# Triangular inverse in 32-column diagonal blocks, its last level as one block, and the triangular product in two parts

## The chip, the cores and the metric

The kernel runs on one core of a Trainium2 chip. The metric is the device time of one launch in microseconds, from the first to the last instruction of the program on that core. Five engines work side by side: TensorE (PE) multiplies matrices and writes to PSUM banks, VectorE (DVE), ScalarE (ACT) and GpSimd (POOL) copy and combine, SyncE (SP) issues the transfers. Each engine takes its instructions in their order and waits on semaphores.

## The reference, cut to what matters

Two layers of a hybrid decoder are run for a prompt of 256 tokens and for 8 samples of 4 tokens: a gated mixing layer with a dense SwiGLU, then an RWKV-7 layer with a top-2-of-8 expert SwiGLU. The change is in the RWKV-7 recurrence, 16 heads of width 64:

```python
def step(s, inp):
    r_t, w_t, k_t, v_t, kk_t, a_t = inp
    s_kk = jnp.einsum("bhij,bhj->bhi", s, kk_t)
    s = (s * w_t[:, :, None, :]
         - s_kk[..., None] * (kk_t * a_t)[:, :, None, :]
         + v_t[..., None] * k_t[:, :, None, :])
    y = jnp.einsum("bhij,bhj->bhi", s, r_t)
    return s, y
```

The kernel doesn't step token by token. It cuts the 256 tokens into four chunks of 64. Within a chunk, the dependence of a token on the tokens before it is a strictly triangular 64x64 matrix per head, and the sequence of steps becomes a product with the inverse of (identity minus that matrix).

## The kernel before, in words

All of the work of this stage stands on one list, `steps`, which every engine's program walks in the same order, each taking its own part of a step. Chunks 0 and 1 lie together as half `i=0`: chunk 0 on partitions 0 to 63 and chunk 1 on partitions 64 to 127; chunks 2 and 3 are half `i=1`. All matrices are 4-byte floats. Each product of the program appears in the trace as two MATMUL records, each with its own weight load.

- `score`: PE makes the products of keys and queries (L1640), DVE masks them into `MS` (L1154). `MS[:, BL]` is the triangular matrix.
- `xt0`: DVE writes the first diagonals into `XT`, the transposed inverse, which starts as the identity (L1162, two instructions of 128 partitions by 512).
- `x0`: PE transposes `XT` into `X` (L1651), ACT copies it out (L801).
- Levels m = 1 to 5 (blocks of 2, 4, 8, 16 and 32) double the size of the diagonal blocks that are inverted: `t1` multiplies the triangular matrix by X (L1663), ACT copies the result to `T1` (L808), `xl` multiplies by X and its transpose (L1678), and DVE writes what belongs to the level over X and XT under a mask (L1170, COPY_PREDICATED). The heads go in two groups of 8, `f` = 0 and 1, so that the engines overlap. Every product is 64x64 by 64x64, in pairs: one for partitions 0 to 63, one for 64 to 127.
- For each chunk c = 0 to 3: `w1` (L1692, L1700), then `u`, which multiplies the inverse by W1 (L1724), then `s` and `y` (L1742, L1751 to L1757). `u` alternates the 64x64 product of its own chunk with a 64x64 product on the other 64 partitions (L1711, L1716), which is needed anyway.

Between two steps of this chain stands one step of the `fill` list: scores of the second half, the same computation for the 32 sample tokens (names that begin with `q_`, some of them 32x32 products: L1779, L1786, L1793), and state updates (`q_s0` L1807, `q_qs` L1816, `q_st` L1865 and L1874).

```python
for i in range(2):
    if i:
        then(("x0", 1))
    for m in range(1, 6):
        then(("t1", i, m))
        then(("xl", i, m))
for c in range(4):
    for kind in ("w1", "u", "s", "y"):
        then((kind, c))
```

The inner line of `u`, for the eight head pairs p of each parity `h2`:

```python
mm = t.matmul(banks[2 + h2][cs, 64 * p:64 * p + 64], XT[cs, i, 2 * p + h2, :], W1[cs, h2, p, :], ...)
...
other(p, 1 - e)
```

After this stage follow the group norm, the output projection (L1913), the routing, and the experts (L1981), which stream 277 MB of weights.

Of the kernel before, what the change touches and what calls it, by code (L numbers as in the profile page):

```python
# [24 lines left out]
I32 = mybir.dt.int32  # L25
# [29 lines left out]
def trunk_kernel(nc, a, out):  # L55

    with ExitStack() as ctx:
# [128 lines left out]
        lvl = view(CHN + 5376, 768, "p (l x t) -> p l x t", l=6, x=2)  # L186
# [6 lines left out]
        id64 = view(CHN + 7200, 64)  # L193
        mskS = view(CHN + 7424, 2 * SMP, "p (r t) -> p r t", parts=2 * SMP, r=2)
# [12 lines left out]
        SB = slice(SMP, 2 * SMP)  # L207
        wkvo = view(CHN + 1024, 512, "p (c j) -> p c j", c=DC)
# [197 lines left out]
        def x_count(i, m, f, x):  # L406

            return 18 * i + 4 * (m - 1) + (2 * f + x if m < 5 else f) + 1
# [41 lines left out]
        def _(sp):  # L450
# [24 lines left out]
            for st in steps:  # L475
                if st == ("xl", 1, 5):
                    sp.wait_ge(S["t1_ready"], 20)
                    stream(len(pieces) - 5, len(pieces) - 4)
# [48 lines left out]
        def _(pool):  # L527
# [60 lines left out]
            step(g.tensor_tensor(lvl, lvlW[:, :, :, 0:64], lvlW[:, :, :, 64:128], ALU.add))  # L588
            step(g.tensor_tensor(id64, ident[:, 0:64], ident[:, 64:128], ALU.add))

# [13 lines left out]
            g.tensor_copy(XT, bc(id64, 1, [P, 2 * H, 64]).rearrange("p (i h) t -> p i h t", i=2)).then_inc(S["masks"], 1)  # L604
            pool.wait_ge(S["masks"], 2)
            g.tensor_copy(XTq[SB], bc(id64[SB, SMP:2 * SMP], 1, [SMP, H, SMP])).then_inc(S["masks"], 1)
# [74 lines left out]
        def _(act):  # L681
# [113 lines left out]
            for st in steps:  # L795
                k = st[0]
                if k == "x0":
                    i = st[1]
                    for f in range(2):
                        act.wait_ge(S["xt_tr"], 2 * i + f + 1)  # L800
                        s_.activation(X[:, 8 * f:8 * f + 8, :], banks[1 + 3 * f][:, :].rearrange("p (h t) -> p h t", h=8),  # L801
                                      ACT.Copy).then_inc(S["x0_ready"], 1)
                elif k == "t1":
                    _, i, m = st
                    n = 5 * i + m - 1
                    for f in range(2):
                        act.wait_ge(S["t1_ready"], 2 * n + f + 1)
                        s_.activation(T1[:, f], banks[3 * f][:, :].rearrange("p (h t) -> p h t", h=8), ACT.Copy) \  # L808
                            .then_inc(S["t1_done"], 1)
# [136 lines left out]
        def _(dve):  # L946
# [200 lines left out]
            for st in steps:  # L1147
# [9 lines left out]
                elif k == "xt0":  # L1157
# [3 lines left out]
                    for f in range(2):  # L1161
                        v.copy_predicated(XT[:, i, 8 * f:8 * f + 8, :], bc(lvl[:, 0, 1, :], 1, [P, 8, 64]).bitcast(I32),  # L1162
                                          MS[:, BL, i, 8 * f:8 * f + 8, :]).then_inc(S["xt0_ready"], 1)
                elif k == "xl":
                    _, i, m = st
                    for f in range(2):
                        for x in range(0 if m < 5 else 1, 2):
                            dve.wait_ge(S["x_ready"], x_count(i, m, f, x))
                            dst = XT[:, i, 8 * f:8 * f + 8, :] if x else X[:, 8 * f:8 * f + 8, :]
                            v.copy_predicated(dst, bc(lvl[:, m, x, :], 1, [P, 8, 64]).bitcast(I32),  # L1170
                                              banks[1 + 3 * f + x][:, :].rearrange("p (h t) -> p h t", h=8)) \
# [30 lines left out]
                elif k == "q_xt0":  # L1202
                    q_wait(dve, "q_ms", 1)
                    v.copy_predicated(XTq[SB], bc(lvl[SB, 0, 1, SB], 1, [SMP, H, SMP]).bitcast(I32), MSq[SB, :, 0, :]) \
                        .then_inc(S["q_dve"], 1)
                elif k == "q_x2":
                    g_ = st[1]
                    q_wait(dve, "q_x2", g_)
                    v.copy_predicated(XTq[SB, 8 * g_:8 * g_ + 8, :], bc(lvl[SB, 1, 1, SB], 1, [SMP, 8, SMP]).bitcast(I32),
# [185 lines left out]
        def _(pe):  # L1395
# [229 lines left out]
            for st in steps:  # L1625
# [19 lines left out]
                elif k == "x0":  # L1645
                    i = st[1]
                    for f in range(2):
                        pe.wait_ge(S["xt0_ready"], 2 * i + f + 1)
                        for j in range(8):
                            for ch in BOTH:  # L1650
# [417 lines left out]
```

## Time and profile before

| | |
|---|---|
| time, median of 3 runs | 1684.76 us (1683.76 to 1685.39) |
| the profiled execution | 1685.16 us, span 1683.3 us |
| PE busy | 1588.4 us (94%) |
| DVE, ACT, POOL busy | 61%, 46%, 5% |
| scores to `x0` of the first half | 614.4 to 621.3 us |
| inverse, both halves | 621.3 to 697.2 us |
| the four chunks' products | 697.2 to about 756 us |
| experts | from 884 us |

A matmul's end is modelled in the trace and its records overlap, so rates of PE are read from the starts of consecutive rows, not from their durations. PEclk is the granted TensorE clock as a share of 2.4 GHz: 1.00 is 2.4 GHz, 0.50 is 1.2 GHz.

### The profile page before, as it was taken

Reading aid. Unit: us, or ns where it says so; the run is one execution under the profiler, and the core shown is the slowest. Engines: PE = TensorE matmul, PEld = TensorE weight load, DVE = VectorE, ACT = ScalarE, POOL = GpSimd, SP = SyncE. Lnnn points to the kernel's source line nnn. Section 1 sums busy time; section 2 is a strip of 40 time slices with the busy share of each in tenths; the row PEclk is TensorE's granted clock in tenths of the full one; section 3 lists DMA queues with packets and bytes.
Section 4 is the critical chain, followed back from the end, with each engine's and each line's share of the span. In section 5 each row is a group of like instructions: output and inputs, shape, how many; then the busy total and the mean of one; then the engine's idle time right before and its main releaser. Section 6 shows DMA issues by size and latency. Waiting matters only on the chain.

```text
span 1683.3 us, 25991 instructions
## 1 busy us (share of the span) xinstructions
PE 1588.4 (94%) x11388; PEld 1258.0 (75%) x11388; DVE 1030.5 (61%) x981; ACT 780.3 (46%) x724; POOL 88.4 (5%) x140
## 2 busy tenths in 40 slices
PE   6999989999989999998869999999999999999991
PEld 5777769999957779995656777777777777777771
DVE  2243134544363645314357888888888888888883
ACT  1120034443331422222026777777777777777771
POOL 2300000000000001232000000000000000000001
PEclk9999999999989999986879999999999999999996
DMA  8443345545333220113039999999999999999963
GB/s 252 130 126 100 107 151 161 164 144 145 104 101 126 75 52 4 32 37 98 25 122 382 404 384 380 367 382 352 379 376 373 376 372 377 365 382 356 379 253 96
DMA packets 238282, 378.28 MB, mean 225 GB/s; under 512 B 27385, under 2 KB 141289, under 8 KB 226610
## 3 DMA queue, kind: packets, MB, share of 16 engines
q1 hardware_dynamic: 232370, 367.19, 62.5%
q0 software_dynamic: 2000, 6.04, 1.2%
q10 hardware_dynamic: 3792, 3.30, 0.6%
q8 instruction: 92, 1.51, 0.4%
q14 instruction: 28, 0.23, 0.0%
HBM read 368.34 MB, written 8.17 MB: 224 GB/s over the span
## 4 chain that ended last, share of the span: by engine, by line
PE 91%; DVE 5%; DMA 2%; issue 1%; ACT 1%; POOL 0%; ACTq 0%; POOLq 0%; DVEq 0%; SPq 0%
PE bank L1981 44%; PE bank L1486 13%; PE bank L1433 8%; PE bank L1532 6%; PE bank L1479 4%; PE bank L1913 2%; PE bank L1678 2%; PE bank L1991 1%; PE bank L1663 1%; PE bank L1470 1%; PE bank L1874 1%; DVE arena L336 1%; PE bank L1865 1%; PE bank L1922 0%; PE bank L1555 0%
## 5 line engine op out<-in xcount | busy, mean ns | idle before, releaser
L1285 DVE TENSOR_TENSOR wL<-ering,wH 128x2048 fp32r<-128x2048 f32 x264 | 604.4, 2290 | 100.1 <-ACT wH L882 95.0
L882 ACT ACTIVATE wH<-ering 128x2048 fp32r<-128x2048 f32 x264 | 506.0, 1917 | 154.9 <-PE bank L1981 154.8
L1981 PE MATMUL bank<-wH,xgH 128*96 128x512 f32 (+1 forms) x768 | 291.0, 379 | 1.2 <-DVE xgL L1292 1.2
L1981 PE MATMUL bank<-wH,xgL 128*96 128x512 f32 (+1 forms) x768 | 288.2, 375 | 0.0
L1981 PE MATMUL bank<-wL,xgH 128*96 128x512 f32 (+1 forms) x768 | 287.8, 375 | 0.0
L1981 PEld LDWEIGHTS bank<-wH,xgH 128*96 128x96 f32 x768 | 126.1, 164 | 44.1 <-DVE xgL L1292 1.5
L1981 PEld LDWEIGHTS bank<-wH,xgL 128*96 128x96 f32 x768 | 124.5, 162 | 44.8
L1981 PEld LDWEIGHTS bank<-wL,xgH 128*96 128x96 f32 x768 | 124.7, 162 | 42.4
L1981 PE MATMUL bank<-wH,hH 128*96 128x512 f32 x352 | 139.3, 396 | 0.0
L1981 PE MATMUL bank<-wH,hL 128*96 128x512 f32 x352 | 138.4, 393 | 0.0
L1981 PE MATMUL bank<-wL,hH 128*96 128x512 f32 x352 | 137.8, 392 | 0.0
L1433 PE MATMUL bank<-arena 128*128 128x288 f32 x512 | 129.4, 414 | 1.2 <-DVE arena L974 1.2
L1028 DVE TENSOR_TENSOR fwL<-fring,fwH 128x2048 fp32r<-128x2048 f32 (+1 forms) x38 | 76.3, 2011 | 80.7 <-ACT fwH L725 80.7
L1433 PEld LDWEIGHTS bank<-arena 128*128 128x128 f32 x512 | 98.4, 194 | 28.5 <-DVE arena L974 1.4
L1532 PE MATMUL bank<-arena 128*128 128x288 f32 (+2 forms) x448 | 112.6, 414 | 1.5 <-DVE arena L1081 1.5
L725 ACT ACTIVATE fwH<-fring 128x2048 fp32r<-128x2048 f32 (+1 forms) x38 | 64.0, 1684 | 104.9 <-DMA fring<-f_w_gate 60.7
L1486 PE MATMUL bank<-fxH,fwH 128*128 128x288 f32 x352 | 105.0, 298 | 7.0 <-DVE fxL L1036 7.0
L1532 PEld LDWEIGHTS bank<-arena 128*128 128x128 f32 (+2 forms) x448 | 82.8, 186 | 30.5 <-issue 4.3
L1486 PE MATMUL bank<-fxH,fwL 128*128 128x288 f32 x352 | 104.5, 297 | 0.0
L1486 PE MATMUL bank<-fxL,fwH 128*128 128x288 f32 x352 | 104.1, 296 | 0.0
L1981 PEld LDWEIGHTS bank<-wH,hL 128*96 128x96 f32 x352 | 56.7, 161 | 24.7
L1981 PEld LDWEIGHTS bank<-wL,hH 128*96 128x96 f32 x352 | 56.9, 162 | 23.0
(342 smaller groups left out, 2018.1 us busy)
## 6 DMA issues: line engine op xcount, KB each, us to landing
ering<-m_w_gate SPq DMA_DIRECT2D x88, 1024.0 KB, 7.7
ering<-m_w_up SPq DMA_DIRECT2D x88, 1024.0 KB, 8.3
ering<-m_w_down SPq DMA_DIRECT2D x88, 1024.0 KB, 7.6
arena<-a_w_in SPq DMA_DIRECT2D x16, 1024.0 KB, 5.4
arena<-b_w_rkv SPq DMA_DIRECT2D x12, 1024.0 KB, 5.1
fring<-f_w_gate SPq DMA_DIRECT2D x11, 1024.0 KB, 5.2
fring<-f_w_up SPq DMA_DIRECT2D x11, 1024.0 KB, 5.3
fring<-f_w_down SPq DMA_DIRECT2D x16, 704.0 KB, 4.7
```

The costliest lines, as they stand in the source:

```text
L336: nc.vector.scalar_tensor_tensor(out=dst[:, c, :], in0=xT[:, c, :], scalar=vec[:, gain + c:gain + c + 1], in1=rinv[:, :], op0=ALU.mult, op ...
L725: nc.scalar.activation(fwH[:, n % FRING, 0:w], fring[:, (F_GU + n) % RING, 0:w], ACT.Copy) \
L882: s_.activation(wH[:, g % HRING, :], ering[:, g % MRING, :], ACT.Copy).then_inc(S["e_hi"], 1)
L1028: v.tensor_tensor(fwL[:, n % FRING, 0:w], fring[:, (F_GU + n) % RING, 0:w], fwH[:, n % FRING, 0:w].bitcast(F32), ALU.subtract).then_inc(S[ ...
L1285: v.tensor_tensor(wL[:, g % HRING, :], ering[:, g % MRING, :], wH[:, g % HRING, :].bitcast(F32), ALU.subtract).then_inc(S["e_lo"], 1)
L1433: mm = t.matmul(banks[g_ % 4][:, 0:T], w[:, k, P * j:P * j + P], hT[:, k, :], start=(k == 0), stop=(k == DC - 1))
L1479: mm = t.matmul(banks[c % 4][:, 0:T], w[:, k, :], vT[:, k, :], start=(k == 0), stop=(k == AC - 1))
L1486: mm = t.matmul(bank[:, 0:T], w2[l], x2[r][:, k, :], start=(start and m == 0), stop=(stop and m == 2))
L1532: mm = t.matmul(bank, w(k), x[:, k, :], start=(k == 0), stop=(k == ks - 1))
L1678: mm = t.matmul(banks[1 + 3 * f + x][ch, 64 * j:64 * j + 64], pair[x], pair[1 - x], start=(j == 0), stop=True, skip_group_check=True)
L1913: mm = t.matmul(banks[c % 4][:, 0:T], w[:, k, P * j:P * j + P], yT[:, k, :], start=(k == 0), stop=(k == DC - 1))
L1981: mm = t.matmul(dst, lhs[l], rhs[r], start=(start and m == 0), stop=(stop and m == 2), skip_group_check=True)
```

## The change

The inverse is kept as two 32x32 diagonal blocks per chunk and head. `XT`, `X` and `T1` are half as wide, and in levels 1 to 4 every 64x64 product becomes two 32x32 products, one for each block; with both chunks that is a round over the four quarters of 32 partitions. Level 5 computes the one off-diagonal block: `t1` is 32 products (32x32), `xl` writes that block and, through the identity, the lower diagonal block side by side into one bank, and DVE copies both in one instruction to the new `XR`. The product `u` is cut in two: rows 0 to 31 of the chunk take a 32x32 product with `XT`, rows 32 to 63 a product of 64 rows by 32 columns with `XR`. `xt0` becomes four instructions of 32 partitions by 512, and PE waits for all four before `x0`. Masks and the counts of the semaphores follow. The samples' steps use a 32-wide identity and are otherwise the same. `steps` is the same list.

```diff
-        XT = view(B[0], 2 * D, "p (i h t) -> p i h t", i=2, h=H)
-        X = view(B[0] + 2048, D, "p (h t) -> p h t", h=H)
-        T1 = view(B[0] + 3072, D, "p (f h t) -> p f h t", f=2, h=8)
+        XT = view(B[0], D, "p (i h t) -> p i h t", i=2, h=H)
+        XR = view(B[0] + 1024, D, "p (i h t) -> p i h t", i=2, h=H)
+        X = view(B[0] + 2048, 512, "p (h t) -> p h t", h=H)
+        T1 = view(B[0] + 2560, 512, "p (h t) -> p h t", h=H)
...
-                    for f in range(2):
-                        v.copy_predicated(XT[:, i, 8 * f:8 * f + 8, :], bc(lvl[:, 0, 1, :], 1, [P, 8, 64]).bitcast(I32),
-                                          MS[:, BL, i, 8 * f:8 * f + 8, :]).then_inc(S["xt0_ready"], 1)
+                    for k4, rows in enumerate(QUARTERS):
+                        o = 32 * (k4 % 2)
+                        v.copy_predicated(XT[rows, i], bc(lvl[rows, 0, 1, :], 1, [32, H, 32]).bitcast(I32),
+                                          MS[rows, BL, i, :, o:o + 32]).then_inc(S["xt0_ready"], 1)
...
+                    if m == 5:
+                        dve.wait_ge(S["x_ready"], x_count(i, 5, 0, 1))
+                        v.tensor_copy(XR[:, i], banks[2][:, :].rearrange("p (h t) -> p h t", h=H)).then_inc(S["x_done"], 1)
+                        continue
...
                         for j in range(8):
-                            for ch in BOTH:
-                                mm = t.matmul(banks[3 * f][ch, 64 * j:64 * j + 64], MS[ch, BL, i, 8 * f + j, :], X[ch, 8 * f + j, :],
-                                              start=(j == 0), stop=True, skip_group_check=True)
+                            for k4, rows in enumerate(QUARTERS):
+                                o = 32 * (k4 % 2)
+                                mm = t.matmul(banks[3 * f][rows, 32 * j:32 * j + 32], MS[rows, BL, i, 8 * f + j, o:o + 32],
+                                              X[rows, 8 * f + j, :], start=(j == 0), stop=True, skip_group_check=True)
...
-                                for ch in BOTH:
-                                    pair = (XT[ch, i, 8 * f + j, :], T1[ch, f, j, :])
-                                    mm = t.matmul(banks[1 + 3 * f + x][ch, 64 * j:64 * j + 64], pair[x], pair[1 - x],
+                                for rows in QUARTERS:
+                                    pair = (XT[rows, i, 8 * f + j, :], T1[rows, 8 * f + j, :])
+                                    mm = t.matmul(banks[1 + 3 * f + x][rows, 32 * j:32 * j + 32], pair[x], pair[1 - x],
                                                   start=(j == 0), stop=True, skip_group_check=True)
...
+                    for j in range(H):
+                        for lhs, to in ((T1, 0), (id32, 32)):
+                            for ch in (0, 64):
+                                rows = slice(ch + 32, ch + 64)
+                                mm = t.matmul(banks[2][ch + to:ch + to + 32, 32 * j:32 * j + 32],
+                                              lhs[rows, j, :] if to == 0 else lhs[rows], XT[rows, i, j, :],
+                                              start=(j == 0), stop=True, skip_group_check=True)
...
                         for p in range(DC):
-                            mm = t.matmul(banks[2 + h2][cs, 64 * p:64 * p + 64], XT[cs, i, 2 * p + h2, :], W1[cs, h2, p, :],
+                            lo, hi = slice(64 * e, 64 * e + 32), slice(64 * e + 32, 64 * e + 64)
+                            t.matmul(banks[2 + h2][lo, 64 * p:64 * p + 64], XT[lo, i, 2 * p + h2, :], W1[lo, h2, p, :],
+                                     start=(p == 0), stop=True, skip_group_check=True)
+                            mm = t.matmul(banks[2 + h2][hi, 64 * p:64 * p + 64], XR[cs, i, 2 * p + h2, :], W1[cs, h2, p, :],
                                           start=(p == 0), stop=True, skip_group_check=True)
                             if p == DC - 1:
                                 mm.then_inc(S["u_ready"], 1)
                             other(p, 1 - e)
```

**A level on PE.** What stands on PE for `t1` and `xl` of the third level of the first half, before (a row gives the bank written, the rows by columns of the output, and the count of equal products behind one another):

```order
L1663 MATMUL bank0<-arena 64x64 x16
L1663 MATMUL bank3<-arena 64x64 x16
L1678 MATMUL bank1<-arena 64x64 x16
L1678 MATMUL bank2<-arena 64x64 x16
L1678 MATMUL bank4<-arena 64x64 x16
L1678 MATMUL bank5<-arena 64x64 x16
```

and now, at the same place:

```order
L1679 MATMUL bank0<-arena 32x32 x32
L1679 MATMUL bank3<-arena 32x32 x32
L1694 MATMUL bank1<-arena 32x32 x32
L1694 MATMUL bank2<-arena 32x32 x32
L1694 MATMUL bank4<-arena 32x32 x32
L1694 MATMUL bank5<-arena 32x32 x32
```

A level of 96 products is one of 192 smaller ones, in the same order of banks.

**The product `u` on PE.** The start of `u` of chunk 0 and its end before; bank 2 and 3 take the product for even and odd heads, banks 4 and 5 the products on the other 64 partitions:

```order
L1840 MATMUL bank7<-arena 32x64 x8
L1724 MATMUL bank2<-arena 64x64
L1711 MATMUL bank4<-arena 64x64
L1724 MATMUL bank2<-arena 64x64
L1711 MATMUL bank4<-arena 64x64
...
L1724 MATMUL bank3<-arena 64x64
L1716 MATMUL bank5<-arena 64x64
L1711 MATMUL bank4<-arena 64x64 x8
```

and now:

```order
L1879 MATMUL bank7<-arena 32x64 x8
L1761 MATMUL bank2<-arena 32x64
L1763 MATMUL bank2<-arena 32x64
L1747 MATMUL bank4<-arena 64x64
L1761 MATMUL bank2<-arena 32x64
L1763 MATMUL bank2<-arena 32x64
L1747 MATMUL bank4<-arena 64x64
...
L1763 MATMUL bank3<-arena 32x64
L1752 MATMUL bank5<-arena 64x64
L1747 MATMUL bank4<-arena 64x64 x8
```

Each of the 16 rounds of a chunk has three products of three sizes (32x32, 64x32 and 64x64 of the array: L1761 has 32 rows of input, L1763 has 64) where it had two of one size.

**`xt0` on DVE.** The second half's `xt0` (L1162) between the masks of the last scores (L1154), the copies of level 3 (L1170) and the samples' first step (L1204), before:

```order
L1154 TENSOR_TENSOR arena<-bank6,arena 128x2x4x64
L1154 TENSOR_TENSOR arena<-bank7,arena 128x2x4x64
L1162 COPY_PREDICATED arena<-arena 128x512 x2
L1170 COPY_PREDICATED arena<-arena,bank1 128x512
L1170 COPY_PREDICATED arena<-arena,bank2 128x512
L1170 COPY_PREDICATED arena<-arena,bank4 128x512
L1170 COPY_PREDICATED arena<-arena,bank5 128x512
L1204 COPY_PREDICATED arena<-arena 32x512
```

and now (L1164, L1173, L1185 and L1219 are the same steps):

```order
L1164 TENSOR_TENSOR arena<-bank6,arena 128x2x4x64
L1164 TENSOR_TENSOR arena<-bank7,arena 128x2x4x64
L1173 COPY_PREDICATED arena<-arena 32x512 x4
L1185 COPY_PREDICATED arena<-arena,bank1 128x256
L1185 COPY_PREDICATED arena<-arena,bank2 128x256
L1185 COPY_PREDICATED arena<-arena,bank4 128x256
L1185 COPY_PREDICATED arena<-arena,bank5 128x256
L1219 COPY_PREDICATED arena<-arena 32x512
```

Two instructions have become four of the same length along the free axis; the copies of a level read and write half as much.

## Rows read from the trace of the kernel before

**Rows 1.** The page's chain of work that ended last, by engine and by line
```profile
PE 91%; DVE 5%; DMA 2%; issue 1%; ACT 1%; POOL 0%; ACTq 0%; POOLq 0%; DVEq 0%; SPq 0%
```

**Rows 2.** Busy time by stretch: A:B length, PE, PEld, DVE, ACT, POOL, then PEclk, DMA, GB/s
```profile
650.30:697.00 46.70, 46.70 (x1553) 46.15 (x1552) 17.59 (x25) 12.63 (x23) 4.17 (x4) 1.00 0.05 15
697.00:734.30 37.30, 37.30 (x1030) 34.52 (x1024) 7.91 (x13) 10.69 (x18) 15.14 (x8) 1.00 0.16 36
...
737.80:741.10 3.30, 3.30 (x72) 3.30 (x70) 0.69 (x1) 0.65 (x2) 1.04 (x1) 0.50 0.02 5
741.30:748.00 6.70, 6.70 (x197) 6.58 (x193) 2.08 (x3) 0.98 (x2) 2.09 (x2) 1.00 0.01 2
748.10:761.60 13.50, 12.82 (x129) 9.98 (x129) 0.29 (x1) 2.37 (x4) 0.53 (x1) 0.50 0.54 175
```

**Rows 3.** Groups of instructions by line, 620 to 702 us: count, busy us, mean ns
```profile
L1678 PE MATMUL bank<-arena 64*64 64x64 f32 x1152 | 35.5, 218 | 0.0
...
L1663 PE MATMUL bank<-arena 64*64 64x64 f32 x640 | 20.8, 219 | 0.2
...
L1651 PE MATMUL bank<-arena 64*64 64x64 f32 x128 | 5.4, 256 | 2.6 <-DVE arena L1162 2.6
```

**Rows 4.** Timeline of PE, 661 to 678 us: start us, length us, what, weights' rows*columns
```profile
669.70 0.69 PE L1779 MATMUL bank<-arena 32*32 32x32 f32 x16
670.31 2.08 PE L1663 MATMUL bank<-arena 64*64 64x64 f32 x64
672.23 1.10 PE L1807 MATMUL bank<-arena 64*64 64x64 f32 x32
673.16 3.90 PE L1678 MATMUL bank<-arena 64*64 64x64 f32 x128
676.99 0.69 PE L1786 MATMUL bank<-arena 32*32 32x32 f32 x16
```

**Rows 5.** Timeline of PE around `u` of chunk 0
```profile
702.20 0.27 PE L1724 MATMUL bank<-arena 64*64 64x64 f32 x1
702.20 0.27 PE L1711 MATMUL bank<-arena 64*64 64x64 f32 x1
...
704.05 0.22 PE L1724 MATMUL bank<-arena 64*64 64x64 f32 x1
704.06 0.22 PE L1716 MATMUL bank<-arena 64*64 64x64 f32 x1
```

**Rows 6.** Timeline of PE, 785 to 800 us, where sizes alternate
```profile
790.13 1.17 PE L1901 MATMUL bank<-arena 128*128 128x288 f32 x2
791.23 1.32 PE L1902 MATMUL bank<-arena 32*128 32x288 f32 x2
792.48 1.33 PE L1897 MATMUL bank<-arena,halves 128*128 128x288 f32 x2
793.60 1.17 PE L1901 MATMUL bank<-arena 128*128 128x288 f32 x2
```

**Rows 7.** Timeline of PE, 811.3 to 816.2 us, where the clock is 0.50
```profile
810.75 5.88 PE L1913 MATMUL bank<-arena 128*128 128x288 f32 x12 [4.31 <-issue]
```

**Rows 8.** Timeline of PE, 613 to 625 us
```profile
614.37 3.72 PE L1640 MATMUL bank<-arena 64*64 64x128 f32 x128 [0.64 <-DVE arena L1146]
618.02 0.65 PE L1767 MATMUL bank<-arena 64*32 64x64 f32 x32
621.27 3.34 PE L1651 MATMUL bank<-arena 64*64 64x64 f32 x64 [2.60 <-DVE arena L1162]
```

**Rows 9.** Timeline of DVE, 620 to 653 us
```profile
620.49 1.34 DVE L1162 COPY_PREDICATED arena<-arena 128x512 f32<-128x512 int32 x2
...
641.75 3.60 DVE L1162 COPY_PREDICATED arena<-arena 128x512 f32<-128x512 int32 x2
645.25 2.55 DVE L1170 COPY_PREDICATED arena<-arena,bank 128x512 f32<-128x512 int32 x4
```

**Rows 10.** Timeline of POOL, 640 to 651 us
```profile
640.51 8.53 POOL L611 TENSOR_TENSOR arena<-arena 32x1024 f32<-32x1024 f32 x4 [24.06 <-PE bank L1640]
```

More of the change, by code:

```diff
@@ L193, in trunk_kernel @@
         id64 = view(CHN + 7200, 64)
+        id32 = view(CHN + 7264, 32)
         mskS = view(CHN + 7424, 2 * SMP, "p (r t) -> p r t", parts=2 * SMP, r=2)
@@ L207, in trunk_kernel @@
         SB = slice(SMP, 2 * SMP)
+        QUARTERS = [slice(32 * k, 32 * k + 32) for k in range(4)]
         wkvo = view(CHN + 1024, 512, "p (c j) -> p c j", c=DC)
@@ L406, in x_count, with t_count @@
         def x_count(i, m, f, x):
-            return 18 * i + 4 * (m - 1) + (2 * f + x if m < 5 else f) + 1
+            return 17 * i + (4 * (m - 1) + 2 * f + x + 1 if m < 5 else 17)
+        def t_count(i, m, f):
+            return 9 * i + (2 * (m - 1) + f + 1 if m < 5 else 9)
         def expert_load(sp, rd, g):
@@ L804, in _ @@
                     _, i, m = st
-                    n = 5 * i + m - 1
-                    for f in range(2):
-                        act.wait_ge(S["t1_ready"], 2 * n + f + 1)
-                        s_.activation(T1[:, f], banks[3 * f][:, :].rearrange("p (h t) -> p h t", h=8), ACT.Copy) \
-                            .then_inc(S["t1_done"], 1)
+                    for f in range(2 if m < 5 else 1):
+                        hs_ = slice(8 * f, 8 * f + 8) if m < 5 else slice(0, H)
+                        act.wait_ge(S["t1_ready"], t_count(i, m, f))
+                        s_.activation(T1[:, hs_, :], banks[3 * f][:, 0:256 if m < 5 else 512].rearrange("p (h t) -> p h t", t=32),
+                                      ACT.Copy).then_inc(S["t1_done"], 1)
                 elif k == "w1":
@@ L1646, in _ @@
                     i = st[1]
+                    pe.wait_ge(S["xt0_ready"], 4 * i + 4)
                     for f in range(2):
-                        pe.wait_ge(S["xt0_ready"], 2 * i + f + 1)
                         for j in range(8):
-                            for ch in BOTH:
-                                mm = t.matmul(banks[1 + 3 * f][ch, 64 * j:64 * j + 64], XT[ch, i, 8 * f + j, :], id64[ch],
+                            for rows in QUARTERS:
+                                mm = t.matmul(banks[1 + 3 * f][rows, 32 * j:32 * j + 32], XT[rows, i, 8 * f + j, :], id32[rows],
                                               start=(j == 0), stop=True, skip_group_check=True)
                         mm.then_inc(S["xt_tr"], 1)
-                elif k == "t1":
+                elif k == "t1" and st[2] < 5:
                     _, i, m = st
@@ L1685, in _ @@
                     if c == 0:
-                        pe.wait_ge(S["x_done"], 36)
+                        pe.wait_ge(S["x_done"], 34)
                         mm = w1_value(0)
@@ L1778, in _ @@
                     for j in range(8):
-                        mm = t.matmul(banks[7][SB, 32 * j:32 * j + 32], XTq[SB, 8 * g_ + j, :], id64[SB, SB],
+                        mm = t.matmul(banks[7][SB, 32 * j:32 * j + 32], XTq[SB, 8 * g_ + j, :], id32[SB],
                                       start=(j == 0), stop=True, skip_group_check=True)
```

49 lines of the change are left out of this document (32 added, 17 removed).

## The prediction, made before the run

> **What bounds the kernel now.** I read the chain that ended last first: it is PE for 91% of the span [rows 1], so what the change adds to PE or takes from it counts, unless PE waits there. Then the stretches of this stage: from 650.3 to 697 us PE is busy for all 46.70 of 46.70 us, and so it is from 697 to 734 us, while DVE has 17.59 and ACT 12.63 us of work in the first of them [rows 2]. So ACT and DVE are covered there, and their smaller copies gain nothing by themselves. The experts behind this stage are on PE's chain too, so a shift here is a shift of the end. The sum is made against the profiled execution, 1685.16 us, 0.4 us above the median of the runs.
>
> **Levels: PE's products.** Before, L1678, L1663 and L1651 have 1152 + 640 + 128 = 1920 records [rows 3]. Their rate is read from starts: L1807 begins at 672.23 and L1678 at 673.16, 0.93 us for 32 records [rows 4], which is 29 ns a record or 58 ns for a pair (one record on each half of the array's rows). 960 pairs at 58.3 ns are 56 us. The change has 3712 records: `x0` 256, `t1` and `xl` of levels 1 to 4 1024 + 2048, level 5 128 + 256. How fast four 32x32 products on four quarters go isn't in the trace, since all its 32x32 products use one quarter. Those take 0.61 us for 16 records from 669.70 to 670.31, a change of size among it; the row's own length less one record's 0.19 leaves 0.50 us for 15 intervals, 32 ns or so [rows 4]. If four quarters run beside one another as two halves do, a round of four records takes that 32 ns. 3584 records in rounds of four are 896, the 128 of the last `t1` are 64 pairs: 960 x 32 ns = 31 us. The gain is 25 us. The other bound is an issue limit. The fastest records of the trace are L1767's, four tiles at a time: 32 in 0.65 less 0.22 us, 14 ns each, but for 32 records only; over 128 records L1640 needs 618.02 - 614.37 = 3.65 us, 28.5 ns each [rows 8]. At 28.5 ns the 3712 records take 106 us, a loss of 50. I take the gain of 25 us, since L1767 shows that products in different tiles do run together, and keep the loss for the range.
>
> **Changes of tile size.** The chip charges for them. L1678 at 673.16 has 128 records, 3.73 us at 58.3 ns a pair, and the next row starts 3.83 us later, 0.10 more. L1779's 16 records take 0.61 where 16 x 32 ns are 0.51. L1663's 64 records take 1.92 where 32 pairs are 1.87 [rows 4]. From 64x64 to 32x32 and back is 0.26 us, 0.13 a change. It holds for single products: L1901, L1902 and L1897 alternate 128-row and 32-row weights, two records each, and a round from 790.13 to 793.60 takes 3.47 us [rows 6]; six records at L1913's 0.49 us (5.88 us for 12 [rows 7]) are 2.94 at most, so two changes cost 0.53, 0.27 each, at half the clock, as 0.13 is at the full one. The Trainium skill, TensorEngine Tiling (Array Packing), "Key Properties", says the same against this change: "Changing tiling mode (not just tile) drains the TensorE". By the page, as by the rows, `u` pays at each product; it gives no price, the rows do.
>
> Around the levels few changes are new: the fill steps of 64x64 now break runs of 32x32, while the samples' 32x32 steps no longer break runs of 64x64. Along PE's order the count goes from 157 to 358, 192 of the 201 new ones in `u`, 9 elsewhere: 1 us.
>
> **The product `u`, where I expect the loss.** Before, L1724 alternates with L1711 or L1716 on the other half of the rows, from 702.20 to 704.11 us for 16 rounds [rows 5]: 0.117 us a round, 4 records, 64 rounds in all. Now a round has 32x32, 64x32 and 64x64 behind one another: six records of 64 columns, none beside another, 6 x 58 = 0.35 us, and three changes of 0.13, together 0.74 us. At the full clock that is 0.62 x 64 = 40 us more. ACT's and DVE's copies behind `u` were hidden by PE work and stay so; nothing else gets shorter.
>
> It won't stay at the full clock, I think. In this same stage the clock is 0.50 from 737.8 to 741.1 us and again from 748.1 to 761.6 [rows 2], after PE had been issuing without a gap, but products of 8 columns or one tile at a time. `u` now uses between a sixteenth and a quarter of the array, with drains. At half the clock a round is 6 x 0.107 + 3 x (0.13 to 0.27), some 1.2 us. With seven rounds of a chunk's 16 at the full clock and nine at half, a chunk's `u` takes 5.2 + 10.8 = 16 us, 14 more than now, 56 us for four. The rest of the stage is about 46 us of PE work, 11 of it at half the clock already; if the clock comes back half-way through what lies between two `u`, it adds some 18 us. Together 75 us, between 40 (clock kept) and about 110 (clock low throughout: 64 x 1.1 + 35).
>
> **`xt0`.** DVE's two L1162 take 1.34 us at 620.49, and PE starts x0 at 621.27 with the first of them done [rows 9, 8]. Four of the same length on 32 partitions each take 0.61 us from start to start (1.34 less one's 0.73), and PE waits for the last: 3 x 0.61 = 1.8 us. In the second half the two took 3.60 us [rows 9], beside POOL's four L611 (8.53 us for four, 2.1 each [rows 10]); each of DVE's, which read SBUF twice, ended only behind one of POOL's. Four would end behind four: 2 x 2.1 = 4.3 us more, and the copies of level 3 (L1185) queue behind them, with PE's next `t1` behind those. PE has run ahead by then, so it waits for all of it. With PE's longer pauses I add 2 us of half clock: 8 us. This is 0 at least (if POOL and DVE don't meet) and 12 at most.
>
> **Sum.** -25 + 1 + 75 + 8 = +59 us: 1685.2 + 59 = 1744, say 1745 us.
>
> **The rivals.**
> - The clock holds: PE still issues without a pause in `u`, and from 650 to 734 us, where half the array or less was in use, it was 1.00 [rows 2]. Then -25 + 1 + 40 + 6 = +22: 1707 us. Against it stand the two stretches at 0.50.
> - An issue limit: the levels run at the 28.5 ns of L1640's 128 records, 75 us more than in the forecast: 1820 us. L1640's records have 128 columns, so their rate can come from their length, and that speaks against it. The Trainium skill, TensorEngine Tiling, "Instruction Overhead", has a rule for such a limit: some 60 cycles for each matmul, so that a tiling factor isn't to be taken from a dimension that is small already. This trace has records at 14 ns in four tiles, below those 25 ns, but not for long.
> - Faster: changes of size inside `u` cost nothing, because what drains is one tile's queue and not the array. Then `u` costs two further serial products a round, 0.117 x 64 = 7.5 us, and the sum is -25 + 1 + 6 + 7.5 = -10.5: 1674 us. It decides the sign when a change costs under about 0.05 us; rows 4 and 6 have 0.13 and more.
>
> **How the numbers follow.** Forecast 0.50 (its own range 1720 to 1775), clock holds 0.12, issue limit 0.24, faster 0.10, and 0.04 for mixtures near no change. 0.2% of the time (3.4 us) is about what a measurement tells from nothing. Faster 0.10, same 0.03, slower 0.87. From 1700 to 1830 us the range takes in the second case and most of the third; out are the faster one and the third's upper end.
>
> **What the profile after would show.** Right: in `u`, the 32-row, 64x32 and 64x64 records start some 60 and 150 ns apart in turn, each chunk's `u` is 12 to 18 us long, and PEclk falls to 0.50 in or behind it; in the levels, four records start within 32 ns and `t1` of a level takes about 1 us; DVE's second `xt0` spans about 8 us. Wrong: a `u` of 2 to 3 us, or a level's `t1` of 3.6 us, or PEclk 0.50 in the levels, which would make their gain nothing and the time up to 30 us longer than forecast.

## The result, and the profile after

The changed kernel takes 1805.9 us (median of 4 runs, 1804.0 to 1806.7) against 1684.3 us (1681.4 to 1685.4): 1.072 times as long, 95% interval 1.0705 to 1.0742. The forecast of slower was right; 1745 us was not: the loss is 121.6 us where 61 were forecast. The measured time lies within the range of 1700 to 1830 us.

The page's chain [rows 1] and its clock row:

```profile
PE 90%; DVE 5%; issue 3%; DMA 2%; ACT 0%; POOL 0%; ACTq 0%; POOLq 0%; DVEq 0%; SPq 0%
...
PEclk9999999999899965566668899999999999999996
```

PE bounds as before. New is that "issue", time in which PE waited for nothing that the profile shows, went from 1% to 3% of the span, and that the clock row reads 5 to 8 for nine slices (of 45 us each) in a row.

Line numbers move: `score` L1640 is now L1655, `x0` L1666, `t1` L1679 (level 5 L1702), `xl` L1694 (L1713), `u` L1761 (32x32) and L1763 (64x32), key and value L1747 and L1752, L1880 is L1919, `xt0` L1173.

Busy time by stretch (columns as in [rows 2]), first of the kernel before, x0 to the first `u` and from there to L1880, then the same two of the kernel after:

```profile
621.30:702.20 80.90, 79.41 (x2537) 77.68 (x2537) 39.52 (x55) 19.77 (x35) 12.46 (x8) 0.98 0.08 21
702.20:772.50 70.30, 67.80 (x1513) 59.47 (x1513) 10.16 (x16) 15.24 (x26) 26.87 (x16) 0.83 0.27 74
```
```profile
626.60:755.30 128.70, 91.59 (x4325) 84.28 (x4326) 32.14 (x54) 14.33 (x33) 12.76 (x8) 0.58 0.05 12
755.30:894.00 138.70, 136.03 (x1645) 101.97 (x1643) 10.24 (x17) 15.25 (x26) 26.89 (x16) 0.63 0.14 37
```

The first scores and x0, PE's timeline [rows 8]:

```profile
617.46 3.72 PE L1655 MATMUL bank<-arena 64*64 64x128 f32 x128 [0.64 <-DVE arena L1156]
...
626.61 1.79 PE L1666 MATMUL bank<-arena 32*32 32x32 f32 x128 [4.84 <-DVE arena L1173]
```

So the 121.6 us by which the two profiled spans differ (1683.3 and 1804.9) fall apart into:

| stretch | before | after | difference | forecast |
|---|---|---|---|---|
| up to the first score | 614.4 | 617.5 | +3.1 | 0 |
| first score to x0 | 6.9 | 9.2 | +2.3 | +1.8 |
| x0 to the first `u` | 80.9 | 128.7 | +47.8 | -25 + 1 + 6 = -18 |
| first `u` to L1880 / L1919 | 70.3 | 138.7 | +68.4 | +75 |
| from there to the end | 910.8 | 910.9 | +0.1 | 0 |

`u` costs about what was forecast. The levels were to gain and lost. The groups by line show how (they answer to [rows 3]), and so do the waits of PE from 610 to 755 us (us in total, times, longest):

```profile
L1694 PE MATMUL bank<-arena 32*32 32x32 f32 x2048 | 31.0, 226 | 25.1 <-issue 25.0
L1679 PE MATMUL bank<-arena 32*32 32x32 f32 x1024 | 16.8, 231 | 8.7 <-issue 8.7
```
```profile
PE bank L1694 <- issue: 25.0, 16, 2.8
PE bank L1679 <- issue: 8.7, 7, 1.8
PE bank L1666 <- DVE arena L1173: 4.8, 1, 4.8
```

In [rows 3] the levels' lines had 0.0 and 0.2 us of idle time. Now PE stands idle for 128.70 - 91.59 = 37.1 us of the stretch, 33.7 of it in 23 pauses in the levels for which no semaphore is to blame. PE's timeline in the levels:

```profile
656.64 1.93 PE L1679 MATMUL bank<-arena 32*32 32x32 f32 x128 [1.01 <-issue]
660.51 1.92 PE L1694 MATMUL bank<-arena 32*32 32x32 f32 x127 [1.93 <-issue]
663.94 2.05 PE L1694 MATMUL bank<-arena 32*32 32x32 f32 x128 [1.51 <-issue]
667.77 0.26 PE L1694 MATMUL bank<-arena 32*32 32x32 f32 x1 [1.78 <-issue]
667.78 1.93 PE L1679 MATMUL bank<-arena 32*32 32x32 f32 x127
671.51 0.25 PE L1679 MATMUL bank<-arena 32*32 32x32 f32 x1 [1.81 <-issue]
```

PE runs 128 records in 1.93 less one record's 0.25 us, 13 ns a record, stops for 1 to 2 us, and runs the next 128: one burst each 3.7 us ((671.51 - 656.64) / 4), whichever line they belong to. That is 29 ns a record on average. The transfers of the same kernel from 650 to 700 us (queue: packets, MB, share of 16 engines):

```profile
q8 instruction: 14, 0.23, 1.9%
```

These are 14 packets of 0.23 MB / 14 = 16 KB in 50 us, one each 3.6 us. A record and its weight load are two instructions; 128 such pairs are 256 instructions, and 16 KB are 64 bytes for each. That q8 carries PE's program shows in its packets over the whole run, first of the kernel before, then of the changed one:

```profile
q8 instruction: 92, 1.51, 0.4%
...
q8 instruction: 107, 1.75, 0.4%
```

Fifteen more packets are 3840 instructions, and PE has 1920 more records and 1920 more weight loads (13308 against 11388). So PE's program comes to it in portions while it runs, and in the levels PE uses up a portion in half the time in which the next one comes. At 29 ns the 4325 records of the stretch take 125 of its 128.7 us. In the kernel before the 2537 records of the stretch would take 74 us at this rate, less than its 80.9, and it has no such pause. The Trainium skill, Runtime: NRT & Kernel Launch, "Instruction fetch mechanics", describes the portions, "16 KiB blocks (256 instructions)", and says that fetching hides because instructions are issued more slowly than they arrive. The trace agrees with the first (16 KB a packet), and not with the second (33.7 us of pauses).

`u` at the full clock and at half, chunk 0:

```profile
756.77 0.29 PE L1761 MATMUL bank<-arena 32*32 32x64 f32 x2
757.00 0.30 PE L1763 MATMUL bank<-arena 64*32 64x64 f32 x2
757.22 0.33 PE L1747 MATMUL bank<-arena 64*64 64x64 f32 x2
757.48 0.29 PE L1761 MATMUL bank<-arena 32*32 32x64 f32 x2
...
763.73 0.41 PE L1761 MATMUL bank<-arena 32*32 32x64 f32 x2
764.07 0.42 PE L1763 MATMUL bank<-arena 64*32 64x64 f32 x2
764.42 0.47 PE L1752 MATMUL bank<-arena 64*64 64x64 f32 x2
764.82 0.41 PE L1761 MATMUL bank<-arena 32*32 32x64 f32 x2
```

A round takes 0.71 us at the clock of 1.00, then 1.09 us at 0.50; forecast were 0.74 and 1.2. Six records of 58 ns leave 0.36 us for three changes of size, 0.12 each; six of 107 ns leave 0.45, 0.15 each.

### The profile page after: what moved, and what is told of

Read it like the earlier page. It is cut to its first block, busy times and chain, and to the rows that moved or that the text cites. A ratio compares the mean times of both kernels' runs of the same rounds, so it can differ in the third digit from the quotient of the medians.

```text
span 1804.9 us, 29832 instructions
## 1 busy us (share of the span) xinstructions
PE 1669.0 (92%) x13308; PEld 1307.3 (72%) x13308; DVE 1025.5 (57%) x983; ACT 774.8 (43%) x722; POOL 87.5 (5%) x143
## 3 DMA queue, kind: packets, MB, share of 16 engines
q1 hardware_dynamic: 232370, 367.19, 58.3%
## 4 chain that ended last, share of the span: by engine, by line
PE 90%; DVE 5%; issue 3%; DMA 2%; ACT 0%; POOL 0%; ACTq 0%; POOLq 0%; DVEq 0%; SPq 0%
PE bank L2020 41%; PE bank L1501 12%; PE bank L1448 7%; PE bank L1547 5%; PE bank L1494 4%; PE bank L1952 2%; PE bank L1694 2%; PE bank L1763 1%; PE bank L2030 1%; PE bank L1761 1%; PE bank L1679 1%; PE bank L1747 1%; PE bank L1485 1%; PE bank L1752 1%; PE bank L1913 1%
## 5 line engine op out<-in xcount | busy, mean ns | idle before, releaser
L2020 PE MATMUL bank<-wL,hH 128*96 128x512 f32 x352 | 137.8, 392 | 0.0
```

What stands on the lines that cost most here:

```text
L2020: mm = t.matmul(dst, lhs[l], rhs[r], start=(start and m == 0), stop=(stop and m == 2), skip_group_check=True)
```

## The experiments

Two theories for the levels. **A**, supply: PE's instructions arrive 16 KB at a time (a portion), each 3.7 us or so, 29 ns for a record with its weight load. **B**, the products' own time, which is what they take with all their instructions there: PEclk is 0.58 in this stretch, and that, with the copies between levels, makes them long. The kernel before ran 1683.8 to 1685.2 us (medians) beside the experiments; ratios are against it.

**1. The levels alone (u_one).**

```diff
-    t.matmul(banks[2 + h2][lo, 64 * p:64 * p + 64], XT[lo, i, 2 * p + h2, :], W1[lo, h2, p, :], ...)
-    mm = t.matmul(banks[2 + h2][hi, 64 * p:64 * p + 64], XR[cs, i, 2 * p + h2, :], W1[cs, h2, p, :], ...)
+    mm = t.matmul(banks[2 + h2][cs, 64 * p:64 * p + 64], U1[cs, i, 2 * p + h2, :], W1[cs, h2, p, :], ...)
```

> The changed kernel with `u` as one 64x64 product a head again; its weights are then a 64-wide view of the memory that holds the diagonal and the upper blocks, so the values are not the inverse's. Levels, copies and all else stay. This gives the price of the split `u` by subtraction. By the forecast's term for `u` (+75 us, 56 inside the four `u` and 18 between them) the time falls to about 1731 us. In the trace of the changed kernel the stretch from the first `u` to L1919 is 138.7 us long against 70.3 before, so if all of that is the split, the time is 1737.5 us. If the low clock at the end of the levels, and not `u`, is what makes this stretch long, it stays above 1770 us.

1733.2 us, ratio 1.0284 (1.0265 to 1.0303). Its stretches, x0 to `u` and behind:

```profile
623.50:750.30 126.80, 90.31 (x4328) 83.09 (x4328) 32.25 (x54) 14.30 (x33) 12.75 (x8) 0.60 0.05 13
750.30:820.80 70.50, 67.75 (x1512) 59.54 (x1512) 10.16 (x16) 15.24 (x26) 26.87 (x16) 0.82 0.28 73
```

From `u` on it is the kernel before again (70.5 us, clock 0.82), so the low clock of the levels carries nothing over. The levels, `xt0` included, cost 48 us.

**2. `u` alone (u_split).**

```diff
-    mm = t.matmul(banks[2 + h2][cs, 64 * p:64 * p + 64], XT[cs, i, 2 * p + h2, :], W1[cs, h2, p, :], ...)
+    t.matmul(banks[2 + h2][lo, 64 * p:64 * p + 64], XT[lo, i, 2 * p + h2, 0:32], W1[lo, h2, p, :], ...)
+    mm = t.matmul(banks[2 + h2][hi, 64 * p:64 * p + 64], XT[cs, i, 2 * p + h2, 32:64], W1[cs, h2, p, :], ...)
```

> The kernel before with only `u` split, into a 32x32 product on the first 32 rows and a 64x32 product on all 64, both read from the 64-wide XT; the result is the reference's. If the split alone makes the loss behind the levels, the time is 1684 + 68 = 1752 us. The forecast's term says 1684 + 75 = 1759. If part of the loss in the changed kernel came from entering `u` at half the clock, it is less here, since before the clock is 1.00 up to `u`: the first `u` then loses about 6 us less, 1746 us.

1750.8 us, ratio 1.040 (1.0375 to 1.0425): the split alone costs 66 us. From its first `u` to L1883 it needs 138.2 us with the clock at 0.63, as the changed kernel does, though its levels ran at 0.98. So the clock at which `u` is entered changes nothing here either. The same products behind the first `u` don't take the same time in every kernel, though: in the profiled runs of the kernels with the split and alternating `u` this stretch is 134.4 to 142.8 us long (xt0_two and cols64), so a few us in the price of `u` are not explained. 48 + 66 = 114 of the 121.6 us; the rest was not separated (3.1 of them lie before the first score, and the two stretches of the profiled run of u_one and of this one are shorter by 1.9 and 0.5 us).

**3. Half the levels' records (two_quarters).**

```diff
-    for rows in QUARTERS:
+    for rows in QUARTERS[::2]:
```

> The changed kernel with x0 and levels 1 to 4 computed on the first and the third quarter of the rows alone: the other two quarters' products are left out, 3328 records become 1664. A round is then two records side by side where it was four, so its own time does not change. Theory A, supply of instructions: PE's instructions come 16 KB at a time, 20 packets and 0.33 MB in 74 us of the levels, and PE stops after each 128 records; then the levels need half the packets, 13 fewer of 3.7 us: 48 us less, 1758 us. Theory B, the clock of 0.50 and the copies that PE waits for between levels: rounds and waits stay, so the time stays within 5 us of 1806.

1772.3 us, ratio 1.0524 (1.0499 to 1.0548): 34 us less than the changed kernel. Its waits of PE, 615 to 720 us:

```profile
PE bank L1679 <- DVE arena L1185: 4.9, 1, 4.9
PE bank L1666 <- DVE arena L1173: 4.8, 1, 4.8
```

DVE's timeline before the first of these waits:

```profile
646.73 8.18 DVE L1173 COPY_PREDICATED arena<-arena 32x512 f32<-32x512 int32 x4
654.94 1.44 DVE L1185 COPY_PREDICATED arena<-arena,bank 128x256 f32<-128x256 int32 x4
```

The stretch x0 to `u`:

```profile
623.80:716.10 92.30, 87.33 (x2663) 83.33 (x2664) 31.97 (x54) 14.35 (x33) 12.75 (x8) 0.51 0.06 15
```

The pauses without a releaser are gone. Theory B's "unchanged" is refuted, theory A's 48 us are not reached: with the supply no longer in the way, PE is at the half clock nearly all through. It is busy for 87.33 us, more than the 77 us that 2663 records need at 29 ns, so the own time decides here. And it waits 4.9 us for L1185, the level's copies, which stand on DVE behind `xt0`'s 8.18 us. That is the wait which the forecast put into `xt0`'s term; in the changed kernel PE was held by its pauses and doesn't show it.

**4. Twice the columns (cols64).** `t1` and `xl` of levels 1 to 4 alike; shown is `xl`.

```diff
-    ... banks[1 + 3 * f + x][rows, 32 * j:32 * j + 32], pair[x], pair[1 - x], ...
+    ... banks[1 + 3 * f + x][rows, 64 * j:64 * j + 64], pair[x], wide[1 - x], ...
```

> The changed kernel with 64 columns instead of 32 in each product of levels 1 to 4: the moving operand also takes the neighbouring head, so the values are not the inverse's; as many instructions, twice the columns. Theory A, supply of instructions: 128 records of 64 columns in rounds of four take 32 x 58 ns = 1.9 us at the full clock and 3.4 us at half, less than the 3.7 us between packets, so the time stays within 5 us of 1806. Theory B, the products' own time at the half clock: 3072 records at 13.4 ns are 41 us and become 82, so the time is 1845 us.

1805.4 us, ratio 1.0712 (1.0694 to 1.0730): the same as the changed kernel, with twice the columns in 3072 records. Its stretch x0 to `u`, and two bursts:

```profile
623.80:752.20 128.40, 90.20 (x4325) 82.38 (x4325) 32.30 (x54) 14.30 (x33) 12.76 (x8) 0.89 0.05 12
```
```profile
694.50 1.98 PE L1697 MATMUL bank<-arena 32*32 32x64 f32 x127 [0.90 <-issue]
698.38 1.36 PE L1697 MATMUL bank<-arena 32*32 32x64 f32 x83 [1.90 <-issue]
```

It is 128.4 us against 128.7, at a mean clock of 0.89 against 0.58, and a burst begins 3.9 us after the last. Neither the columns nor the clock sets this stretch with all its records in place, and theory B's 1845 us are out. What is left is the number of records.

**5 and 6. Fewer columns in the kernel before, with the count kept and halved (b_cols32, b_one128).** `x0` and `t1` are changed in the same way as the `xl` shown.

```diff
-    mm = t.matmul(... 64 * j:64 * j + 64], pair[x], pair[1 - x], ...)
+    mm = t.matmul(... 64 * j:64 * j + 32], pair[x], pair[1 - x][:, 0:32], ...)   # b_cols32
```
```diff
-    for ch in BOTH:
-        pair = (XT[ch, i, 8 * f + j, :], T1[ch, f, j, :])
-        mm = t.matmul(banks[1 + 3 * f + x][ch, 64 * j:64 * j + 64], pair[x], pair[1 - x], ...)
+    pair = (XT[:, i, 8 * f + j, :], T1[:, f, j, :])
+    mm = t.matmul(banks[1 + 3 * f + x][0:64, 64 * j:64 * j + 32], pair[x], pair[1 - x][:, 0:32], ...)
```

> The kernel before with 32 columns instead of 64 in each product of x0 and of all levels: the right half of each 64x64 result is left out, the 1920 records stay. Theory A, supply of instructions: 16 KB, which is 128 records with their weight loads, reach PE each 3.7 us or so, 29 ns a record, and that is what the levels of the kernel before take already (58.3 ns a pair). So half the columns gain nothing: within 4 us of 1685. Theory B, the products' own time: a pair goes from 58.3 ns to the 32 ns of 32-column products, 960 pairs, 25 us less: 1660 us.

> As the kernel before, but in x0 and all levels one product of 128-row weights and 32 columns takes the place of the pair of 64-row products of 64 columns; the second chunk's results are left out. The 1920 records become 960. Theory A: the supply then allows 29 ns a record, 960 x 29 = 28 us, and their own time is 960 x 32 = 31 us, against 56 before: 25 us less, 1660 us, where the same halving of columns with the count kept gains nothing. Theory B (own time alone) says 1660 us here too; only the other kernel of this pair tells them apart. If 128-row weights of 32 columns cost more than 32 ns a record, less is gained.

Both expectations failed: 1705.8 us, ratio 1.0137 (1.0108 to 1.0165), and 1744.1 us, 1.0361 (1.0338 to 1.0384). Both are slower, clear of the noise, with less work. First rows of b_cols32, at the full clock and at half, then of b_one128 at half:

```profile
636.18 1.94 PE L1663 MATMUL bank<-arena 64*64 64x32 f32 x62
...
702.80 3.60 PE L1678 MATMUL bank<-arena 64*64 64x32 f32 x64
```
```profile
705.45 3.62 PE L1661 MATMUL bank<-arena 128*64 128x32 f32 x32
```

62 records in 1.94 less 0.22 us are 28 ns each, a pair 56 ns, as with 64 columns; at half the clock 64 records in 3.38 us are 53 ns, a pair 107. In b_one128 a record takes (3.62 - 0.25) / 31 = 109 ns, where 32 columns at half the clock were to take 64. Two records that follow each other in one tile are spaced by the 64 columns of their weights, not by the 32 that move. L1779, from which the forecast read its 32 ns, has weights of 32 columns. The Trainium skill, TensorE: Matmul & The Clock Gate, "LDWEIGHTS (loading the stationary operand)", says that a weight load takes its number of columns / 1.2 in ns; an estimate by it is 53 ns for 64 columns. The 56 ns at the full clock agree, the 107 at half are twice that. The loss goes with the clock: between x0 and `u` it is 0.74 in b_cols32 and 0.51 in b_one128, against 0.98. The pair says nothing on A, since a product's own time never fell.

**7 and 8. More instructions, no more work (b_waits, b_waits_long).**

```diff
+    for _ in range(9):                       # b_waits: ahead of each pair in the levels
+        pe.wait_ge(S["masks"], 2)
+    for _ in range(14):                      # b_waits_long: ahead of each product of L1433
+        pe.wait_ge(S["h_ready"], DC)
```

> The kernel before, with nine waits ahead of each pair of products in the levels, all on a semaphore that has long had its value: 1814 more instructions for PE there, and no other work. Theory A, supply of instructions (16 KB, 256 instructions, each 3.7 us): the levels stand at that limit already with 29 ns a record, so 1814 more are 7.1 portions more and the time grows by 26 us to 1710 us, with pauses of PE that show no releaser. Theory B: there is no such limit, the levels run at the products' own time, and a wait that is met is passed while products run: within 4 us of 1684.

> The control: the kernel before, with 1792 more met waits, this time seven for each product of L1433, whose 512 records of 288 columns take 411 ns each. Theory A: 128 records there take some 50 us, far longer than the 3.7 us a portion, so the extra seven portions are hidden: within 4 us of 1684. If a met wait costs PE's sequencer time that products don't hide, this kernel is slower as well, and the other one's loss says nothing on the supply.

1843.2 us, ratio 1.0943 (1.0923 to 1.0964), and 1753.0 us, 1.0408 (1.0388 to 1.0427). The control is slower too, so the pair says nothing for A. (Two waits share an instruction: fourteen are the seven that the expectation speaks of.) A met wait, one whose semaphore has its value already, costs PE 68 us / 1792 = 38 ns even ahead of products of 400 ns. Between the short ones the loss is 158 / 1814 = 87 ns for each, but that isn't the wait's price alone: the clock there is 0.53 from 650 to 700 us, against 1.00 in the kernel before. In b_waits, q8 brought fewer portions in 650 to 700 us than in the changed kernel, not more:

```profile
q8 instruction: 6, 0.10, 0.7%
```

**9. The products of `u` in another order (u_grouped).**

```diff
     for p in range(DC):
         t.matmul(banks[2 + h2][lo, ...], XT[lo, ...], W1[lo, h2, p, :], ...)
+    for p in range(DC):
         mm = t.matmul(banks[2 + h2][hi, ...], XR[cs, ...], W1[cs, h2, p, :], ...)
         ...
+    for p in range(DC):
         other(p, 1 - e)
```

> The changed kernel with the products of `u` in another order: for each half of the heads first the eight 32x32 ones, then the eight 64x32 ones, then the eight of key or value; the same products, some 24 changes of tile size where there were 192. In the trace of the changed kernel a round of `u` takes 0.705 us at the full clock, 0.36 of it in three changes, and 1.095 us at half, 0.45 of it in three changes: 0.12 and 0.15 us a change. If changes cost that, 168 fewer are 20 to 25 us: 1783 us. By the forecast's prices (0.13 to 0.27) it is 22 to 45 us less. If the drain belongs to the tile that changes and the loss is the serial products alone, the time stays at 1806 us.

1761.4 us, ratio 1.0469 (1.0444 to 1.0495): 44.5 us less than the changed kernel with the very same products. Its `u` and the stretch from the first `u` to the state transposes:

```profile
795.45 1.08 PE L1761 MATMUL bank<-arena 32*32 32x64 f32 x16
796.45 1.08 PE L1764 MATMUL bank<-arena 64*32 64x64 f32 x16
797.46 0.97 PE L1752 MATMUL bank<-arena 64*64 64x64 f32 x13
```
```profile
749.10:849.00 99.90, 96.86 (x1646) 85.97 (x1645) 10.16 (x16) 15.26 (x26) 26.89 (x16) 0.73 0.19 52
```

Sixteen records of a kind (eight products) take 1.00 us, 63 ns each, so a round is 0.38 us where it was 0.71. That is 21 us for 64 rounds at the full clock. The stretch is 38.8 us shorter; the rest of it goes along with the clock, 0.73 against 0.63, and was not measured apart. "The loss is the serial products alone" is refuted: most of it comes from alternating the sizes, by the changes themselves and by the lower clock together.

**10. The same order in the kernel before (b_u_grouped).** The diff is that of u_split, in the order of u_grouped.

> The kernel before with `u` split, its products grouped by tile size: eight 32x32, eight 64x32, eight of key or value, for each half of the heads. The result is the reference's. Split and alternating it was 1750.8 us. If grouping takes off what it took off in the changed kernel (44.5 us), the time is 1706 us. If only the changes of size themselves are saved (168 at 0.12 to 0.15 us), and the clock doesn't follow, it is 1728 us. The serial products alone, 1.0 us a group of eight at the full clock, six groups against 1.9 us in all before, are 4.3 us a chunk, 17 us, 1702 us: the least it can be.

1713.4 us, ratio 1.0178 (1.0160 to 1.0196), 37 us less than u_split. The split with few changes of size costs 28.5 us: more than the 17 of the products in a row. From its first `u` to L1885, 702.5 to 802.5 us, the clock is 0.73, where it was 0.83 in the kernel before; how much of the 11 us that makes wasn't measured apart.

**11. `xt0` in two instructions (xt0_two).**

```diff
-    for k4, rows in enumerate(QUARTERS):
-        v.copy_predicated(XT[rows, i], ..., MS[rows, BL, i, :, o:o + 32])
+    for f in range(2):
+        v.copy_predicated(XT[:, i, 8 * f:8 * f + 8, :], ..., MS[:, BL, i, 8 * f:8 * f + 8, 0:32])
```

> The changed kernel with `xt0` in two instructions of 128 partitions for each half of the chunks, as before, in place of four of 32 partitions; two of the four quarters then copy the wrong columns of MS. The forecast gave the four instructions 8 us: 1798 us. In the trace of the changed kernel PE waits for them in the first half alone, and scores to x0 takes 9.15 us against 6.9; in the second half PE's stops show no releaser, and DVE is done before PE gets there. By that the time is 2 us less, 1804 us.

1795.9 us (1794.4 to 1803.1), ratio 1.0682 (1.0650 to 1.0714), which overlaps that of the changed kernel. The time alone is nearer to the forecast's 8 us (1798) than to 2 us (1804), but the trace doesn't show these 8 at their place: first score to x0 is 7.0 us, 2.2 less, and x0 to `u` is 128.3 against 128.7. Of the 12.2 us by which its span is shorter (1792.7 us), 2.2 lie before the first score, 4.3 behind the first `u` and 3.2 behind L1918, where nothing was changed; why is open.

**12. Half the records with twice the columns (two_cols64).** The diffs of experiments 3 and 4 together.

> The changed kernel with x0 and levels 1 to 4 on the first and third quarter alone and with 64 columns in each product of levels 1 to 4: half the records, as many columns in all as the changed kernel has. It asks where 14 us of the 48 expected of the halved count went (measured 34). In that kernel the clock was 0.50 through the levels, a pair took 54 ns, and the 64x64 steps between the levels ran at half speed too. With 64 columns a pair takes 58 ns at the full clock, so the levels' own records take no longer. If it was the clock, which also slows the steps in between, then PEclk is near 1.00 here and the time falls from 1772 to 1758 to 1766 us. If it was PE's one wait of 4.9 us on DVE and things like it, the time stays within 3 us of 1772. If the products' own columns set the levels' time at all, this kernel is no faster than the changed one with all four quarters, 1806 us.

1803.3 us, ratio 1.0712 (1.0690 to 1.0733): the last of the three answers. It corrects what experiment 4 seemed to say, that columns and clock don't matter. The stretch x0 to `u`, and PE's longest run of L1697:

```profile
623.50:750.10 126.60, 126.57 (x2663) 121.61 (x2664) 32.08 (x54) 14.33 (x33) 12.76 (x8) 0.51 0.04 10
```
```profile
691.80 6.71 PE L1697 MATMUL bank<-arena 32*32 32x64 f32 x122
```

PE has no pause at all, and the clock stays at 0.51, against the 1.00 that I had assumed. The 122 records have 121 intervals in 6.71 less one record's 0.31 us, 53 ns each, which is slower than the supply. So these stretches take the longer of the two, own time or supply: with four quarters and 64 columns the own time is 14 ns at the full clock (experiment 4's burst of 127 records in 1.98 us) and the supply's 29 ns decide; with two quarters at half the clock it is 53 ns, and they decide. That this comes out near experiment 4's time is a coincidence of two limits. What took experiment 3's 14 us is thus not measured by this one; its clock of 0.51 and its one wait of 4.9 us remain as the candidates.

## Why the prediction was wrong, point by point

- **Levels, -25 us: this step failed.** "If four quarters run beside one another as two halves do, a round of four records takes that 32 ns." In the bursts they do run side by side, 13 ns a record even at half the clock, 53 ns a round of four. But the instructions of 3712 records don't arrive at that rate. The text had the other bound beside it, 28.5 ns for each of L1640's 128 records, 106 us, a loss of 50; it was set aside because L1640's rate "can come from their length". What the runs showed in its place: the levels with `xt0` lose 48 us by themselves (experiment 1), at 29 ns a record, set by the number of records (experiments 3 and 4). That this is the 16 KB portions of q8 is read from the traces, from the pauses after each 128 records and the packets; no run changed the supply alone (experiments 5 to 8 were to test it and could not). The rival "issue limit", at 0.24, named this rate and 1820 us, 14 above the measured time. Its mechanism was only half right: it isn't a limit on each instruction, since the bursts are twice as fast, but one on what is supplied over some microseconds. The rows gave a warning: the rates of records in small tiles came from 0.50 us (L1779) and 0.43 us (L1767), much shorter than the 3.7 us of one portion.
- **Which of them it was could not be read from [rows 3, 4].** The kernel before takes 29 ns a record in runs of 64x64 products, by its own 58.3 ns a pair, and that is the supply's rate as well. With other work between them its stretch stands a little above the supply's limit (80.9 us against 74), without pauses. So close to both limits, it had little to gain from smaller products unless there were fewer of them, and the change has nearly twice as many. This is worked out; no run shows it.
- **Changes of size around the levels, +1 us:** not seen apart from the pauses.
- **`u`, +75 us: right, a little high.** It is 66 us when added alone, 72.7 when taken back out (1805.9 - 1733.2), 68.4 us in the trace. The price of a change, 0.13, was 0.12 at the full clock; at half it was 0.15, where 0.27 was the upper end. Chunk 0's `u` takes 14.6 us (755.35 to 769.9), forecast 16. That the clock would fall in `u` was right and counted: 0.63 against 0.83.
- **`xt0`, +8 us: right in DVE's rows, too much on PE.** In the first half x0 starts 2.3 us later after the scores (1.8 forecast). In the second DVE took as long as forecast, but PE was held by the supply and didn't wait for it:

```profile
657.06 8.18 DVE L1173 COPY_PREDICATED arena<-arena 32x512 f32<-32x512 int32 x4
665.27 1.10 DVE L1185 COPY_PREDICATED arena<-arena,bank 128x256 f32<-128x256 int32 x3
```

- **"PEclk 0.50 in the levels, which would make their gain nothing":** the clock did fall, to 0.58, but by experiment 4, with the same time at 0.89, it costs nothing there.
- **The faster rival** asked for changes of size that cost nothing in `u`; experiment 9, without most of them, takes back 44.5 of `u`'s 72.7 us, the clock's part included.

With 106 us for the levels the sum would have been 1685.2 + 50 + 1 + 75 + 8 = 1819, and with `xt0` at its measured 2.3 us 1813, against 1806. Each of the other terms was off by less than 10 us, on the high side; the levels' was off by some 70, from -25 to the 45.9 of experiment 1's stretch (126.8 - 80.9).

## What to carry to other kernels

Before cutting products into smaller ones, count instructions: in these traces a PE record with its weight load needed about 29 ns of supply on average, however fast its tile is, so a long run of them gains nothing below that. Here the first pause came 161 records after x0 began. Look at PE's pauses marked "issue", at whether they stand behind each 128 records, and at the packets of the instruction queue; "issue" alone doesn't tell, since b_waits has such pauses too (2.6 us in 13), with 6 packets in 50 us on q8. A rate read from a stretch shorter than one portion (3.7 us) needn't hold for a long one. And where products of several tile sizes must be made, put those of one size together: the same products took 44.5 us less for 168 fewer changes.

## What was not expected of the hardware

- **The supply of instructions:** one 16 KB portion each 3.6 us or so at the fastest. From 650 to 700 us the changed kernel and cols64, which pause, have 14; the kernel before and two_quarters, which don't, have 13 and 12. Why a portion takes 3.7 us isn't shown.
- **Weights set the spacing:** products of 64x64 and 128x64 weights are no faster with 32 moving columns than with 64 (64x64: 56 ns a pair at the full clock; at half 107 ns for 64x64, 109 for 128x64).
- **A busy PE can stand at half its clock:** in two_cols64 PE was busy for 126.57 of 126.60 us, on two of the four quarters, and the granted clock was 0.51; in cols64, on all four and with pauses for 30% of the time, it was 0.89. And with half the moving columns the levels of the kernel before went from 0.98 to 0.74.
- **A met wait isn't free on PE:** 38 ns ahead of long products, where there are seven such instructions in a row. The 512 records of L1433 start within 203.5 us there (20.0 to 223.5), within 137.8 in the kernel before.
